# Sparse attention of a two-block transformer kernel: heads taken in pairs, one of each key group, on both halves of the TensorE array

## What is computed

```python
def nsa_mixer(q, k_c, v_c, k_s, v_s, k_w, v_w, gate_logits, positions, ...):
    G, Hg, dh = NSA_KV_GROUPS, HEADS_PER_GROUP, HEAD_DIM      # 2, 4, 64
    ...
    kc = compress_tokens(k_c, ...)                             # 31 compressed keys
    vc = compress_tokens(v_c, ...)
    s_c = jnp.einsum('btghd,bcgd->bghtc', qg, kc) * scale
    p_c = masked_softmax(s_c, (c_start + CMP_BLOCK - 1)[None, :] <= t_idx[:, None])
    o_cmp = jnp.einsum('bghtc,bcgd->btghd', p_c.astype(vc.dtype), vc)
    ...
    o_slc = lax.map(sel_chunk, jnp.arange(T // SEL_Q_CHUNK))   # selected blocks
    o_win = lax.map(win_block, jnp.arange(T // WIN_Q_BLOCK))   # window of 512 keys
    g = jax.nn.sigmoid(gate_logits).reshape(B, T, G, Hg, 3)
    out = g[..., 0:1] * o_cmp + g[..., 1:2] * o_slc + g[..., 2:3] * o_win
```

## Time and profile before

| | us |
|---|---|
| median of 3 runs | 2760.3 (2758.71 to 2762.12) |
| the profiled execution | 2757.09 |
| its span, first to last instruction | 2755.1 |
| PE busy, of the span | 2448.9 (89%) |
| DVE busy | 1448.1 (53%) |
| ACT busy | 685.3 (25%) |
| POOL busy | 610.8 (22%) |

### The profile page before, as it was taken

How to read it: one execution, slowest core, us unless ns; L and a number is a source line. 1 busy time by engine, 2 the same in 40 slices (tenths; PEclk the granted TensorE clock), 3 DMA queues, 4 the chain that set the end, 5 groups by cost and what they waited for, 6 DMA issues and landing times.

```text
span 2755.1 us, 23152 instructions
## 1 busy us (share of the span) xinstructions
PE 2448.9 (89%) x7690; PEld 1252.7 (45%) x7690; DVE 1448.1 (53%) x3802; ACT 685.3 (25%) x1633; POOL 610.8 (22%) x567
## 2 busy tenths in 40 slices
PE   6999999999999999999969898888888878788886
PEld 2456554435554455444644444444433334343332
DVE  0010331135531956431167677777777767677775
ACT  2000013116411133421224322223222222222222
POOL 0002000010000000000024443444444434344441
PEclk9999999999999979899989999999999999999999
DMA  7102241100012100012269999999999999999996
GB/s 322 61 31 99 118 194 49 61 0 1 38 61 85 71 31 31 5 57 86 83 243 404 401 416 422 421 422 422 421 422 421 421 422 420 422 421 422 421 421 271
DMA packets 83942, 657.18 MB, mean 239 GB/s; under 512 B 9410, under 2 KB 9698, under 8 KB 11378
## 3 DMA queue, kind: packets, MB, share of 16 engines
q0 software_dynamic: 75904, 552.21, 48.5%
q1 hardware_dynamic: 7922, 103.50, 9.7%
HBM read 653.58 MB, written 2.10 MB: 238 GB/s over the span
## 4 chain that ended last, share of the span: by engine, by line
PE 57%; DMA 28%; DVE 9%; issue 2%; ACT 2%; POOL 0%; DVEq 0%; POOLq 0%; PEldq 0%; ACTq 0%
DMA arena<-in_peer_uv,newton 27%; PE psum L561 22%; PE psum L1132 11%; PE psum L631 3%; DVE arena L2128 2%; PE psum L938 2%; PE psum L955 2%; PE psum L1074 1%; PE psum L611 1%; PE psum L777 1%; PE psum L1101 1%; PE psum L727 1%; PE psum L971 1%; PE psum L946 1%; PE psum L785 1%
## 5 line engine op out<-in xcount | busy, mean ns | idle before, releaser
L1132 PE MATMUL psum<-arena 128*128 128x512 f32 x2048 | 981.7, 628 | 217.9 <-ACT arena L1485 214.6
L2128 DVE CUSTOM_DVE_ANT_0 arena<-arena 128x1024 f32<-128x1024 f32 x512 | 620.9, 1224 | 284.7 <-DMA arena<-in_peer_uv,newton 279.3
L2286 POOL DMA_INDIRECT arena<-in_peer_uv,newton x512 | 568.0, 1109 | 812.1 <-PE psum L1132 704.7
L1132 PEld LDWEIGHTS psum<-arena 128*128 128x128 f32 x2048 | 398.9, 200 | 711.3 <-issue 706.4
L561 PE MATMUL psum<-arena 128*128 128x512 f32 (+3 forms) x1568 | 604.2, 546 | 11.5 <-DVE arena L1657 3.6
L561 PEld LDWEIGHTS psum<-arena 128*128 128x128 f32 (+1 forms) x1568 | 294.3, 189 | 319.1 <-issue 307.5
L1193 ACT ACTIVATE arena<-psum 128x512 f32<-128x512 f32 (+11 forms) x311 | 166.7, 545 | 723.4 <-PE psum L561 308.5
L1485 ACT ACTIVATE arena<-ident,newton 128x128 f32<-128x128 f32 x512 | 177.8, 394 | 268.4 <-DVE newton L2137 253.6
L1476 ACT ACTIVATE arena<-arena 128x2 f32<-128x2 f32 (+1 forms) x258 | 52.5, 203 | 665.2 <-DVE arena L2128 661.3
L1101 PE MATMUL psum<-arena 128*128 128x256 f32 x512 | 129.3, 379 | 0.7 <-DVE arena L1732 0.5
L1101 PEld LDWEIGHTS psum<-arena 128*128 128x128 f32 x512 | 97.0, 190 | 62.2 <-issue 54.8
(11 more groups left out here) (299 smaller groups left out, 2029.3 us busy)
## 6 DMA issues: line engine op xcount, KB each, us to landing
arena<-in_weights SPq DMA_DIRECT2D x48, 2048.0 KB, 9.0
arena<-in_peer_uv,newton POOLq DMA_INDIRECT x512, 26.5
arena<-in_xin POOLq DMA_DIRECT2D x1, 3072.0 KB, 17.6
arena<-in_dft_l POOLq DMA_DIRECT2D x1, 2048.0 KB, 15.5
arena<-in_cmp_w POOLq DMA_DIRECT2D x1, 2048.0 KB, 7.5
out<-arena SPq DMA_DIRECT2D x4, 512.0 KB, 11.8
arena<-in_pool_band POOLq DMA_DIRECT2D x1, 1280.0 KB, 5.7
arena<-in_fnet_w POOLq DMA_DIRECT2D x1, 1024.0 KB, 22.3
```

The lines of the kernel that those rows point to most:

```text
L1132: ins = mm(bank(j_y[t][q]), DIAG[i % 4], ROW[ROW_PLACE[i]][:, D + 512 * q:D + 512 * q + 512], start=first, stop=last)
L2128: v.tensor_tensor_reduce(out=u, in0=u, in1=HNT[ITEM_TILE[i // 16]][:, :], scale=1.0, scalar=0.0, op0=ALU.mult, op1=ALU.add, accum_out=DOTS ...
L2286: g.indirect_dma_start(out=ROW[ROW_PLACE[i]][:, :], out_offset=None, in_=a["peer_uv"], in_offset=bass.IndirectOffsetOnAxis(ap=IDX[:, n, e: ...
```

## The change

Heads are taken in pairs, head `jj` of group 0 with head `jj` of group 1. Items are numbered so that 2p and 2p+1 are the same query tile and branch of the two heads of a pair, and all loops run over 32 pairs.

- `scores2(p)` claims both banks 0 and 1, then issues the matmul on rows 0 to 63 and the one on rows 64 to 127 next to each other.
- `values2(p)` alternates lower and upper columns for each key tile, as `values1` does.
- The order of a PE step becomes: scores of pair p+2, two transposes, values of pair p-1, memory steps. Before, an item had: transpose, values of item i-2, memory step, scores of item i+4.
- The compressed branch runs once per pair of heads (4 times in place of 8). Its scores are 31 columns wide; those of group 1 wait by a new semaphore `cmp_first` until those of group 0, which go to the same bank, have ended. Its transposes are matmuls with the identity on alternating column halves. `PC` grows to 8 x 32.
- DVE: one scaling of maxima and one reciprocal per pair in place of two; `weigh2(p)` waits for the exponentials of both items. Two convolution taps per pair, pairs 0 to 15.
- The side work moves to the pair of the old item, but for `norm_sum` (pairs 17 and 22), `center` (17), `variance` (22), `inverse` (23), `scale` (24), silu (25).

```diff
-        ITEMS2 = [(hh, qt, br) for hh in range(8) for qt in range(4) for br in range(2)]
+        ITEMS2 = [(2 * jj + g, qt, br) for jj in range(4) for qt in range(4) for br in range(2) for g in range(2)]
...
-            def cmp_scores(hh):
-                jj, g = HEAD2[hh]
-                j = j_cs[hh]
-                claim(pe, j)
+            def cmp_scores(jj, g):
+                j = j_cs[jj]
+                if g == 0:
+                    claim(pe, j)
+                else:
+                    pe.wait_ge(S["cmp_first"], jj + 1)
                 r = 64 * g
                 for qt in range(4):
-                    ins = mm(bank(j, P, P * qt), QN[r:r + 64, jj, qt * P:(qt + 1) * P], KCT[r:r + 64, :],
+                    ins = mm(bank(j, N_CMP, 32 * (4 * g + qt)), QN[r:r + 64, jj, qt * P:(qt + 1) * P], KCT[r:r + 64, 0:N_CMP],
                              start=True, stop=True)
...
+                for qt in range(4):
+                    for g in range(2):
+                        ins = mm(bank(j, P, qt * P, p0=64 * g, p1=64 * g + N_CMP), PC[:, 4 * g + qt, 0:N_CMP], ident[:, :],
+                                 start=True, stop=True)
...
+            def scores2(p):
+                for i in (2 * p, 2 * p + 1):
+                    claim(pe, j_s2[i])
+                for i in (2 * p, 2 * p + 1):
+                    hh, qt, br = ITEMS2[i]
+                    jj, g = HEAD2[hh]
+                    r, n = 64 * g, (qt + 1) * P
+                    src = KW if br else KS
+                    q = QR[r:r + 64, jj, qt * P:(qt + 1) * P]
+                    done(mm(bank(j_s2[i], n), q, src[r:r + 64, 0:n], start=True, stop=True), j_s2[i])
...
-            def values2(i):
-                hh, qt, br = ITEMS2[i]
-                jj, g = HEAD2[hh]
+            def values2(p):
+                hh, qt, br = ITEMS2[2 * p]
                 jo = j_o2[hh // 2]
-                read_out(pe, [j_pt2[i]])
+                last = p % 8 == 7
+                read_out(pe, j_pt2[2 * p:2 * p + 2])
                 for kt in range(qt + 1):
-                    ins = mm(bank(jo, P, qt * P, p0=64 * g, p1=64 * g + 64), VSW[:, kt, P * br + 64 * g:P * br + 64 * g + 64],
-                             PT2[:, i % 4, kt * P:(kt + 1) * P], start=False, stop=(i % 8 == 7 and kt == qt))
-                if i % 16 == 15:
+                    for g in range(2):
+                        ins = mm(bank(jo, P, qt * P, p0=64 * g, p1=64 * g + 64), VSW[:, kt, P * br + 64 * g:P * br + 64 * g + 64],
+                                 PT2[:, (2 * p + g) % 4, kt * P:(kt + 1) * P], start=False, stop=(last and kt == qt))
...
             scores2(0)
+            cmp_scores(0, 0)
+            cmp_scores(0, 1)
             scores2(1)
-            cmp_scores(0)
-            scores2(2)
-            scores2(3)
-            for i in range(64):
-                transpose2(i)
...
+            for p in range(32):
+                if p < 30:
+                    scores2(p + 2)
...
+                transpose2(2 * p)
+                transpose2(2 * p + 1)
...
+                if p >= 1:
+                    values2(p - 1)
+                if p == 17:
                     norm_sum(j_ln_cv[0][0], CACC, 0, L, 4, S["conv_y"], 0)
...
+                memory_step(2 * p)
+                memory_step(2 * p + 1)
+            values2(31)
...
+            def weigh2(p):
+
+                c = 2 * p % 8
+                dve.wait_ge(S["p_exp"], 2 * p + 2)
+                link(v.reciprocal(rinv[:, c:c + 2], rsum[:, c:c + 2]))
...
+            for p in range(32):
+                weigh2(p)
+                if p < 30:
+                    masked_max(p + 2)
+                if p % 8 == 2 and p < 24:
+                    cmp_shift(p // 8 + 1)
+                if p < 16:
+                    conv_taps(2)
+
+                if p % 8 == 4 and p < 24:
+                    cmp_normalise(p // 8 + 1)
```

More of the change, by code:

```diff
@@ L455, in build @@
         j_o2 = [None] * 4
[L456 to L465, removed]
+        for jj in range(4):
+            j_o2[jj] = J.take(6 + jj % 2)
+            j_cs[jj] = J.take(5)
+            j_cpt[jj] = J.take(5)
+        j_ln_cv_var = J.take(5)
+        for i in range(64):
+            j_s2[i] = J.take(i % 2)
+            j_pt2[i] = J.take(3 + i % 2)
         j_mk += [J.take(2) for _ in range(4)]
@@ L894, in _ @@
             for g in range(2):
[L895 to L896 removed]
+                mm(bank(j_vct[0], 64, 64 * g, p0=64 * g, p1=64 * g + N_CMP), ones[0:1, 0:N_CMP], rows[0:1, 0:64], start=True, stop=False)
+                ins = mm(bank(j_vct[0], 64, 64 * g, p0=64 * g, p1=64 * g + N_CMP), HD[:, 1, N_CMP * g:N_CMP * (g + 1)], CMPW2[:, 1, :],
                          start=False, stop=True)
@@ L930, in scores2 @@
-            def scores2(i):
-                hh, qt, br = ITEMS2[i]
[L932 to L938, removed]
+                if g == 0:
+                    ins.then_inc(S["cmp_first"], 1)
+                else:
+                    done(ins, j)
@@ L1394, in _ @@
             exp2(0)
+            exp2(1)
             cmp_exp(0)
[L1396 to L1407, removed]
+            for p in range(32):
+                for i in (2 * p + 2, 2 * p + 3):
+                    if i < 64:
+                        exp2(i)
+                for i in (2 * p, 2 * p + 1):
+                    transposed2(i)
+                if p == 0:
+                    cmp_pt(0)
+                if p % 8 == 3 and p < 24:
+                    cmp_exp(p // 8 + 1)
+                if p % 8 == 5 and p < 24:
+                    cmp_pt(p // 8 + 1)
+                if p in (6, 8, 10, 12):
+                    copy_out(j_mk[p // 2 + 1], MK[:, p // 2 + 1, :], LC)
+                if p == 18:
                     squares(SQ2, CACC, 0, L, 4, S["centered"], 24)
-                if i == 43:
+                if p == 22:
                     root(j_ln_cv[1][0], RS2[:, :], L)
-                if i in (32, 50):
-                    copy_out(j_mv[i // 50], MV[:, i // 50, 0:512])
-                if i == 49:
+                if p in (16, 25):
+                    copy_out(j_mv[p // 25], MV[:, p // 25, 0:512])
+                if p == 25:
                     for c in range(4):
@@ L1928, in cmp_normalise @@
                 link(v.reduce_sum(csum[:, :], PC[:, :, 0:N_CMP], axis=AX))
                 link(v.reciprocal(csum[:, :], csum[:, :]))
-                link(v.tensor_tensor(csum[:, :], csum[:, :], gates_tok[:, :, 3 * head], ALU.mult))
-                link(v.tensor_scalar(csum[:, 0:1], csum[:, 0:1], vc("cmp_valid"), None, ALU.mult))
+                for g in range(2):
+                    ins = v.tensor_tensor(csum[:, 4 * g:4 * g + 4], csum[:, 4 * g:4 * g + 4], gates_tok[:, :, 3 * (4 * g + jj)],
+                                          ALU.mult)
@@ L1933, in cmp_normalise @@
+                link(ins)
+                for g in range(2):
+                    ins = v.tensor_scalar(csum[:, 4 * g:4 * g + 1], csum[:, 4 * g:4 * g + 1], vc("cmp_valid"), None, ALU.mult)
+                link(ins)
                 v.tensor_tensor(PC[:, :, 0:N_CMP], PC[:, :, 0:N_CMP],
-                                csum[:, :].rearrange("p (t o) -> p t o", o=1).to_broadcast([P, 4, N_CMP]), ALU.mult)\
+                                csum[:, :].rearrange("p (t o) -> p t o", o=1).to_broadcast([P, 8, N_CMP]), ALU.mult)\
```

164 lines of the change are left out of this document (79 added, 85 removed).

## The result

The changed kernel takes 2694.6 us in the median of four runs (2692.4 to 2696.5); the kernel before, run beside it, 2759.5. The ratio is 0.9766, with a 95% interval of 0.9749 to 0.9783: 64.9 us faster. The forecast was 2714.3, a gain of 46, and its range ended at 2699.0.

The account below looks back on a forecast made before the run. PE was taken to set the pace, with 98 us of room on DVE. The terms -19 - 15 - 4 - 12.5 + 0 + 4.5 = -46 took 2760.3 to 2714.3 us; its own range was 2704 to 2722, the wider one 2699 to 2734.

Parts of the forecast that it names:

- Scores, -15: Score matmuls of a head pair on row halves: partial overlap saves 15 us, with bounds 0 and -23.5.
- three steps in place of four: Pair's scores, two passes a head: only second head's first pass overlaps first head's second; 32 us for all pairs.
- the cheap bound: Scores of a pair: the second head costs nothing, 23.5 us for 32 pairs, a saving of 23.5.
- the prediction's own sign: Sign of being right: a lone pair of scores at 512 keys takes about 1.5 us, not 2.1 or 1.05.
- The rival that took its price from one matmul: Scores: both heads stream side by side from the first pass, -8.5 us more, 2705.8 us; chance 0.1.
- Values, -19: Values of a pair in alternation on column halves: 25.0 us in place of 44.3, bounds 0 and -22.
- 2n + 1: Values: steps of 0.107 us for a pair of n key tiles, the second head starting one pass later, plus 0.14 us.
- Compressed branch, -4: Compressed branch run per pair: scores -1, transposes -0.5, values -2.4 us, in all -4 (0 to -8).
- Clock in the middle, -12.5: Mid-stage half-clock stretch around the centring: PE idles 1.5 us for 4.8, no fall; 27.3 us of work takes 14.6.
- a sign that the prediction itself had named as wrong: Sign of being wrong: a clock of 0.5 after pair 18 or in pairs 24 to 31.
- Clock at the start, 0: Half-clock stretch at the stage's start: about as long as before, with about the same work, 0 (-4 to +4).
- Waits, +4.5: Waits left in the stage, from the loop of maxima and scores and ACT's silu: +4.5 us (0 to +15).

Follow-up runs that it names:

- The cut-up centring: Kernel before, with the convolution's centring cut into its four instructions, one in each of items 35 to 38: 2750.2 us beside 2760.4, ratio 0.9971.
- The two waits: Changed kernel, the second head of each pair waiting for the first: in scores 2731.7 us, in values (issued head by head) 2718.7, in both 2755.1.

## Why the prediction was right and where it fell short

- **Which engine, and the term's kind.** PE set the pace, DVE's room was real, and 69.1 us less of PE's busy time made the stage 62.9 us shorter. The next stages moved as they were. Right.
- **Scores, -15.** This is the step that failed. It said that the second head's first pass runs beside the first head's second, "three steps in place of four". Pairs cost 0.42, 0.63, 0.84 and 1.07 us, what one item does; the term is -23.5, the cheap bound, 8.5 us more. By the prediction's own sign a lone pair at 512 keys was to take 1.5 us. The rival that took its price from one matmul was the right one, and the rule of the Trainium skill (TensorE: Matmul & The Clock Gate, Measured speedup vs the span model) agrees here with the trace: 0.63 us for the pair at 256 keys, 0.63 for one.
- **Values, -19.** The same step: 2n + 1 was wrong, 2n is right, -22.0. The row was there to see it: 0.36, 0.58, 0.80, 1.03 grow by 0.22 a tile, which gives 0.14 + 6 x 0.22 = 1.46 for one head's six tiles, and the pair in the first block took 1.46. The prediction took 0.107 for a pass from the scores' rows, not 0.11 from the values' own, and filled the difference with a step that does not exist.
- **Compressed branch, -4.** Measured in the chain: 4 x (0.81 + 1.02 + 1.00 + 1.00) = 15.3 us against 21.4, -6.1. The values' three steps were again two.
- **Transposes, no term.** The sum left them out, without a reason. A pair's cost 0.15 us less side by side than two items' apart, as the chain shows for two and four tiles; for 32 pairs that is -4.8, by estimate. This is the second step that failed.
- **Clock in the middle, -12.5.** The size was right and its reason was not, so a good part of it is luck. 37.5 us at half in the whole stage in place of 64.8, as forecast, is worth 12.7. The reason was that an idle of 1.5 us in place of 4.8 would not let the clock fall. PE idled 1.8 us in place of 3.1, and the clock fell: a sign that the prediction itself had named as wrong. The cut-up centring shows that a shorter standstill can keep the clock up in the order before. In the new order it came back after 3.4 us, and that is what saved the time; the waits show that this goes with the overlap of the scores, since without it the same place cost 23.9 us at half after an idle of 1.5. The prediction had no link between the overlap and the clock.
- **Clock at the start, 0.** 30.7 us in place of 37.5, with two short falls later; the sum of the forecast held, its places did not.
- **Waits, +4.5.** PE's idle time in the stage rose by 6.2 us. The size was about right. The silu cost 4.2 us in place of up to 3; the loop of maxima and scores was reckoned with scores that are too dear.
- **The sum** of the terms as measured is -23.5 - 22.0 - 6.1 - 4.8 - 12.7 + 6.2 = -62.9, the 62.9 us by which the stage became shorter. That it meets so closely is in part chance, since the clock's term takes the whole stretches as work.
- **The range** took the cheapest scores, but held each wrong step for an error of its own. Scores, values and compressed values rested on one assumption about passes, and failed together: 8.5 + 3.0 + about 2 us of the 19. The transposes are 4.8 more. The waits took 1.7 back, and some 2 us lie between the profiled runs and the medians.

The two waits bear the account out: 34.9 us for the rows and 21.9 for the columns, 58.3 together, against 64.9 for the whole change. Of the 34.9, up to 19 is the clock, by the estimate above.

Still open is why the clock follows the scores. The runs say that it comes back sooner with overlapped scores and no later without overlapped values; they don't say why. No run takes the overlap of the compressed branch away.

## What to carry to other kernels

Two small matmuls on different halves of the array, rows or columns, cost what one costs, as long as they stand next to each other in the program; strict alternation is needed only for long runs of each. Before pricing an overlap, fit one head's own rows first and see what the pair's row leaves over. List every kind of work that the new order puts side by side, the transposes here too, and not only the kinds that the change is about. The chain says what the end hung on, not what the other engines did meanwhile: how long an engine stood still is read from its own timeline or waits (here 3.1 and 4.2 us, where the chain suggested 4.8 and 8). When several terms rest on one assumption, move them together in the range. And where the clock is at half in some stretches, a change that makes PE's matmuls overlap may bring it back sooner: look for that gain, or for its loss when they are pulled apart.

## What the hardware showed

- Passes of a second head ran beside three to four passes of the first that had been issued ahead of them: two tiles a head, issued head by head, took 0.59 us, like in alternation, four took 1.51, between 1.02 and about 1.9.
- TensorE stayed at 0.50 for 37.5 us while it was busy for 35.9 of them, with the scores of a pair one after the other; with the scores side by side the stretches were 30.7, 27.3 or 13.7 us at the start and 3.4 to 6.8 in the middle, where runs with separate scores had 23.9 to 27.3. The idle of PE ahead of the middle stretch was 1.8 us with 3.4 us at half, and 1.5 us with 23.9.
- A wait of one matmul for another on the same engine, through a semaphore, cost 0.10 to 0.11 us: 0.04 without work, and 0.06 more in the piece behind it (1.03, then 1.09).
- Transposes of two items cost 0.15 us less side by side than apart: 1.02 us for 8, against twice 0.59.
